# Expert jobs of 160 rows without bias products on TensorE, with bias columns and row folds on GpSimd

## The reference

```python
xb = h[row_tok].reshape(n_blocks, EXPERT_BLOCK, D)      # rows gathered by expert
hid = jnp.dot(xblk, w1[e]) + b1[e]                      # 1024 -> 2048, with a bias
glu = jnp.minimum(hid[:, 0::2], SWIGLU_LIMIT)
lin = jnp.clip(hid[:, 1::2], -SWIGLU_LIMIT, SWIGLU_LIMIT)
act = glu * jax.nn.sigmoid(SWIGLU_ALPHA * glu) * (lin + 1.0)
out = jnp.dot(act, w2[e]) + b2[e]                       # 1024 -> 1024, with a bias
y = zeros((T, D)).at[row_tok].add(out * row_gate)       # scattered back with the gate
```

## Time and profile before

| | |
|---|---|
| median of three runs | 2200.66 us (2197.22 to 2201.60) |
| the profiled execution | 2203.66 us, of which the span from first to last instruction is 2202.1 us |
| TensorE busy in the span | 2050.6 us, 93% |
| DVE, ACT, GpSimd busy | 1600.1, 1296.1 and 423.2 us |
| mean granted TensorE clock | 0.974 |
| loop of jobs | from 675 to about 2170 us |

### The profile page before, as it was taken

How to read it: one execution, slowest core, us unless ns; L and a number is a source line. 1 busy time by engine, 2 the same in 40 slices (tenths; PEclk the granted TensorE clock), 3 DMA queues, 4 the chain that set the end, 5 groups by cost and what they waited for, 6 DMA issues and landing times. The chain is left out here.

```text
span 2202.1 us, 40266 instructions
## 1 busy us (share of the span) xinstructions
PE 2050.6 (93%) x11606; PEld 1763.0 (80%) x11607; DVE 1600.1 (73%) x2206; ACT 1296.1 (59%) x1869; POOL 423.2 (19%) x478
## 2 busy tenths in 40 slices
PE   7999977778957999999999999999999999999994
PEld 6888867777846878889798897979898888979883
DVE  5342176985657677878878787888788797887876
ACT  5221245563436576766757667677667676675765
POOL 3100000220241131221213121132212131121311
PEclk9999989999978999999999999999999999999997
DMA  5221210004247897979889798899898797988978
GB/s 182 61 82 58 67 68 1 11 20 159 96 156 254 278 305 243 352 247 327 287 278 333 237 353 267 297 314 358 253 318 302 257 349 248 334 284 278 331 239 309
DMA packets 260913, 506.10 MB, mean 230 GB/s; under 512 B 34496, under 2 KB 35520, under 8 KB 260566
## 3 DMA queue, kind: packets, MB, share of 16 engines
q1 hardware_dynamic: 243064, 458.05, 60.5%
q0 software_dynamic: 17792, 47.33, 8.8%
q10 hardware_dynamic: 4, 0.02, 0.0%
HBM read 466.10 MB, written 39.22 MB: 229 GB/s over the span
## 5 line engine op out<-in xcount | busy, mean ns | idle before, releaser
L1820 DVE TENSOR_TENSOR wlo<-raw,whi 128x1024 fp32r<-128x1024 f32 x774 | 932.1, 1219 | 75.6 <-ACT whi L1296 67.7
L1296 ACT ACTIVATE whi<-raw 128x1024 fp32r<-128x1024 f32 x775 | 846.1, 1116 | 221.6 <-PE ps L981 162.8
L979 PE MATMUL ps<-xT,whi 128*128 128x320 f32 x1920 | 525.2, 350 | 5.6 <-DMA brow<-brow_d 5.0
L981 PE MATMUL ps<-xT,wlo 128*128 128x160 f32 x1920 | 456.4, 238 | 0.0
L979 PEld LDWEIGHTS ps<-xT,whi 128*128 128x128 f32 x1920 | 364.0, 190 | 10.0 <-issue 6.6
L981 PEld LDWEIGHTS ps<-xT,wlo 128*128 128x128 f32 x1920 | 369.8, 193 | 0.2
L2088 POOL DMA_INDIRECT acc_d<-y,icur x64 | 102.6, 1604 | 947.9 <-ACT y L1330 885.3
L621 PE MATMUL ps<-whi,xT 128*128 128x512 f32 x544 | 216.0, 397 | 0.0
L621 PE MATMUL ps<-whi,aT 128*128 128x512 f32 x512 | 213.1, 416 | 1.3
L623 PE MATMUL ps<-whi,xT 128*128 128x512 f32 x544 | 213.3, 392 | 0.0
L622 PE MATMUL ps<-wlo,xT 128*128 128x512 f32 x544 | 213.1, 392 | 0.0
(11 more groups left out here) (300 smaller groups left out, 3484.4 us busy)
## 6 DMA issues: line engine op xcount, KB each, us to landing
raw<-in_w SPq DMA_DIRECT2D x780, 512.0 KB, 7.4
raw<-in_w_in SPq DMA_DIRECT2D x16, 512.0 KB, 4.7
xs<-in_x SPq DMA_DIRECT2D x8, 512.0 KB, 10.5
raw<-in_w_out SPq DMA_DIRECT2D x8, 512.0 KB, 3.9
mix<-in_x SPq DMA_DIRECT2D x8, 512.0 KB, 4.2
acc_d<-mix SPq DMA_DIRECT2D x8, 512.0 KB, 5.0
h_d<-h SPq DMA_DIRECT2D x8, 512.0 KB, 2.6
mix<-acc_d SPq DMA_DIRECT2D x8, 512.0 KB, 7.5
```

The lines of the kernel that those rows point to most:

```text
L979: pe.matmul(o2, wh[:, a, cols], xT2[:, :, k, 0:JOB_T], start=q == 0 and a == 0, stop=False, skip_group_check=True)
L981: m = pe.matmul(o, wl[:, a, cols], xT2[:, 0, k, 0:JOB_T], start=False, stop=q == QUARTERS - 1 and a == 1, skip_group_check=True)
L1296: act.activation(parted(slot(whis, s)), paired(raw_slot(s), s), ACT.Copy).then_inc(split_hi, 1)
L1820: dve.tensor_tensor(parted(slot(wlos, s)), paired(raw_slot(s), s), parted(slot(whis, s).bitcast(F32)), ALU.subtract).then_inc(split_lo, 1)
```

## The change

It has four parts.

1. In wide jobs the four bias products per c (L984) go. Instead, before the loop, SP loads `b1` once as 32 rows (`b1r`), TensorE turns it in 16 small transposes, and DVE copies the result to `bcolT`, with 1 added to the second half. Per job GpSimd copies one expert's 16 columns to `bcur`. ACT adds the gate's bias inside the sigmoid, which takes two instructions of 160 columns instead of one of 320. DVE gets one more instruction of 320 columns per c, which adds the bias to `lsum`.
2. The bias row for narrow jobs is no longer loaded by SP at the end of its list (nor by ACT the first time) but by GpSimd on its own queue, once the up-projection of the job before is over (`next_bias`).
3. `y_fold` moves from DVE to GpSimd: ACT scales all 64 rows of the second bank into `y` in one instruction, GpSimd copies rows 32 to 63 to `yfold`, then adds them to rows 0 to 31. In GpSimd's list both folds stand ahead of the first scatter.
4. GpSimd reads the next job's expert number from the table (one more register load per job).

The diff, cut:

```diff
+            sp.dma_start(b1r[:, :], b1[0]).then_inc(b1r_in, 16)
...
-                    wait(quarter_used, j * NS + 4 * (DENSE_UNITS + 4))
-                    wait(brow1_in, j * 16 + 16)
-                    sp.dma_start(brow[0:2, 0:2 * FF].bitcast(F32),
-                                 bias_part(en, slice(0, 2 * FF))).then_inc(brow1_in, 16)
...
+            pe.wait_ge(b1r_in, 16)
+            for two in range(2):
+                for i in range(BTILES):
+                    cols = slice(2 * P * i + two, 2 * P * (i + 1) + two - 1, 2)
+                    m = pe.transpose(ps[:, 3, (two * BTILES + i) * NE:(two * BTILES + i + 1) * NE],
+                                     b1r[:, cols], ident[0:NE, 0:NE])
+            m.then_inc(bias_turned, 1)
...
-                        if q == 0:
-                            pe.matmul(o, brow[:, c * UNIT + 256 * odd + P * i:c * UNIT + 256 * odd + P * (i + 1)], ones2[:, 0:JOB_T],
-                                      start=False, stop=False, skip_group_check=True)
...
                     act.wait_ge(sum_taken, j * 8 + 2 * c + 1)
-                    act.activation(sigw[:, :, :], gsum[:, :, :], ACT.Gelu_apprx_sigmoid).then_inc(sig_set, 1)
+                    if c == 0:
+                        act.wait_ge(bcur_set, j + 1)
+                    for i in range(2):
+                        m = act.activation(sigw[:, i, :], gsum[:, i, :], ACT.Gelu_apprx_sigmoid,
+                                           bias=bcur[:, 0, 2 * c + i:2 * c + i + 1])
+                    m.then_inc(sig_set, 1)
...
-                    act.wait_ge(y_set[1], j * 2 + c - 3)
-                    act.activation(yfold[:, c - 4, :], ps[HALF:2 * HALF, out_bank(2, c, 1), :], ACT.Copy,
-                                   scale=gcur[HALF:2 * HALF, 1:2]).then_inc(yfolded, 1)
+                    act.activation(y[0:2 * HALF, 1, (c - 4) * UNIT:(c - 3) * UNIT], ps[0:2 * HALF, out_bank(2, c, 1), :], ACT.Copy,
+                                   scale=gcur[0:2 * HALF, 1:2]).then_inc(yfolded, 1)
...
-            act.wait_ge(quarter_used, 4 * DENSE_UNITS)
-            act.dma_start(brow[0:2, 0:2 * FF].bitcast(F32), bias_part(0, slice(0, 2 * FF))).then_inc(brow1_in, 16)
...
+                if c == 0:
+                    dve.wait_ge(bcur_set, j + 1)
+                dve.tensor_tensor(lsum[:, :, :], lsum[:, :, :],
+                                  bcur[:, 1, 2 * c:2 * c + 2].unsqueeze(2).broadcast_to([P, 2, JOB_T]),
+                                  ALU.add).then_inc(lin_biased, 1)
+                dve.wait_ge(lin_biased, j * 4 + c + 1)
...
+            def next_bias(j, e):
+
+                wait(quarter_used, j * NS + 4 * (DENSE_UNITS + 4))
+                wait(brow1_in, j * 16 + 16)
+                pool.dma_start(brow[0:2, 0:2 * FF].bitcast(F32), bias_part(e, slice(0, 2 * FF))).then_inc(brow1_in, 16)
+                wait(act_set, j * 4 + 4)
+                columns(bass.ds(e, 1))
+                wait(bcur_set, j + 2)
+
+            def y_fold(j, c):
+
+                wait(yfolded, j * 2 + c - 3)
+                cols = slice((c - 4) * UNIT, (c - 3) * UNIT)
+                pool.tensor_copy(yfold[:, c - 4, :], y[HALF:2 * HALF, 1, cols]).then_inc(low_moved, 1)
+                pool.wait_ge(low_moved, j * 2 + c - 3)
+                pool.tensor_tensor(y[0:HALF, 1, cols], y[0:HALF, 1, cols], yfold[:, c - 4, :], ALU.add).then_inc(y_set[1], 1)
+                pool.wait_ge(y_set[1], j * 2 + c - 1)
...
                 pool.tensor_copy(icur[:, :], ikept[:, :]).then_inc(tcur_set, 1)
                 wait(tcur_set, j + 1)
 
+                if blocks == 2:
+                    next_bias(j, e)
+                    y_fold(j, 4)
+                    y_fold(j, 5)
                 for b in ((0, 1) if blocks == 2 else (1, 0)):
+                    if b == 0 and blocks == 1:
+                        pool.sem_inc(low_moved, 2)
+                        next_bias(j, e)
                     if b < blocks:
                         wait(y_set[b], j * 2 + 4)
```

More of the change, by code:

```diff
@@ L81 @@
 B_AV, B_HI, B_HG, B_OUT = 0, 128, 640, 1152
+BTILES = FF // P
 F32 = mybir.dt.float32
@@ L150, in build @@
     tinit = at("tinit", B + 68 * KB, [P, PAD_ROWS, 2])
+    b1r = at("b1r", B + 40 * KB, [NE, 2 * FF])
     hf = at("hf", B, [P, HH, T])
@@ L180, in build @@
     glw = at("glw", B + 55.75 * KB, [P, 2, 2, JOB_T])
+    bcur = at("bcur", B + 58.25 * KB, [P, 2, BTILES])
     yfold = at("yfold", B + 60 * KB, [HALF, 2, UNIT])
+    bcolT = at("bcolT", B + 64 * KB, [P, 2, BTILES, NE])
     R = [B + 72.5 * KB]
@@ L328, in build @@
         rooted, eps_set, brow_zero = sem("rooted"), sem("eps_set"), sem("brow_zero")
-        lin_set, yfolded = sem("lin_set"), sem("yfolded")
+        lin_set, yfolded, low_moved = sem("lin_set"), sem("yfolded"), sem("low_moved")
+        b1r_in, bias_turned, bcolT_set, bcur_set = (
+            sem(n) for n in ("b1r_in", "bias_turned", "bcolT_set", "bcur_set"))
+        lin_biased = sem("lin_biased")
         pool_mark, sync_mark, act_mark = sem("pool_mark"), sem("sync_mark"), sem("act_mark")
@@ L1887, in aT_wide @@
                                   aTh[:, k, 1, 0:HALF].bitcast(F32), ALU.subtract).then_inc(aT_lo, 1)
-            def y_fold(j, c):
-                dve.wait_ge(yfolded, j * 2 + c - 3)
-                dve.scalar_tensor_tensor(out=y[0:HALF, 1, (c - 4) * UNIT:(c - 3) * UNIT], in0=ps[0:HALF, out_bank(2, c, 1), :],
-                                         scalar=gcur[0:HALF, 1:2], in1=yfold[:, c - 4, :],
-                                         op0=ALU.mult, op1=ALU.add).then_inc(y_set[1], 1)
             def job(j, blocks):
@@ L1899, in job @@
                         (hidden if blocks == 1 else hidden_wide)(j, UNIT_END[s - 1])
-                    if blocks == 2 and UNIT_END.get(s - 1, 0) == 4:
-                        y_fold(j, 4)
                     jsplit(j, s + AHEAD)
@@ L1911, in job @@
                 if blocks == 2:
-                    y_fold(j, 5)
                     dve.sem_inc(hid_taken, 4)
@@ L1916, in job @@
                     dve.sem_inc(lin_set, 4)
+                    dve.sem_inc(lin_biased, 4)
             for s in range(4):
                 jsplit(0, s)
+            dve.wait_ge(bias_turned, 1)
+            dve.tensor_copy(bcolT[:, 0, :, :], ps[:, 3, 0:BTILES * NE].rearrange("p (i e) -> p i e", e=NE))
+            dve.tensor_scalar(bcolT[:, 1, :, :], ps[:, 3, BTILES * NE:2 * BTILES * NE].rearrange("p (i e) -> p i e", e=NE),
+                              1.0, None, ALU.add).then_inc(bcolT_set, 1)
             dve.memset(y[:, 1, :], 0.0).then_inc(y_zero, 1)
@@ L2039, in _ @@
                     pool.wait_ge(brow_zero, 2)
+                    pool.dma_start(brow[0:2, 0:2 * FF].bitcast(F32), bias_part(0, slice(0, 2 * FF))).then_inc(brow1_in, 16)
                     link(pool.memset(xg[:, 1, :], 0.0))
@@ L2067, in gather, with columns @@
                                             ).then_inc(gathered, 16)
+            def columns(e):
+                pool.tensor_copy(bcur[:, :, :], bcolT[:, :, :, e].rearrange("p a i o -> p a (i o)")).then_inc(bcur_set, 1)
+            def next_bias(j, e):
[12 more added lines that the diff above has]
+                pool.wait_ge(y_set[1], j * 2 + c - 1)
             def job(j, blocks):
@@ L2074, in job @@
                 load_slots(pool.value_load(jobt[0:1, 1, bass.ds(j + 1, 1)], min_val=0, max_val=NE * JOBS_E - 1))
+                e = pool.value_load(jobt[0:1, 0, bass.ds(j + 1, 1)], min_val=0, max_val=NE - 1)
                 wait(x_turned, j * 4 + 4)
@@ L2107, in _ @@
             pool.wait_ge(y_zero, 1)
+            pool.wait_ge(bcolT_set, 1)
+            columns(slice(0, 1))
+            pool.wait_ge(bcur_set, 1)
             with pool.Fori(0, JOBS, 1) as j:
```

## The result

| | before | changed |
|---|---|---|
| median | 2199.30 us (4 runs, 2197.22 to 2201.60) | 2170.60 us (4 runs, 2168.57 to 2173.04) |
| ratio, 95% interval | | 0.9861 [0.9848, 0.9873] |
| span of the profiled execution | 2202.1 us | 2168.5 us |
| mean granted TensorE clock | 0.974 | 0.974 |
| TensorE, DVE, GpSimd busy | 2050.6, 1600.1, 423.2 us | 2023.1, 1630.9, 534.9 us |

The kernel is 1.4% faster. The forecast was 2186 us, 0.67% faster: right in sign, but with a gain of 14.7 us where 28.7 us were measured. The time lies inside the range only because the range took in the first rival (2166 to 2170 us), which had 20%.

The account below looks back on a forecast made before the run. TensorE, busy 93% of the span, was taken as the bound, full in wide jobs. Terms -27 - 7.7 + 20 + 0.4 = -14.3 us took the profiled 2203.66 to 2189.4 us, a median forecast of 2186 us, range 2167 to 2200.

Parts of the forecast that it names:

- the first rival: Narrow jobs behind wide ones: gathers stay in time, loss only 0 to 4 us, time 2166 to 2170 us; chance 20%.
- The forecast's case: Late gathers cost TensorE 20 us at its turns in narrow jobs; own range 2172 to 2196 us, chance 62%.
- The bias products (-27): Wide jobs' up-projection: removing 240 products from TensorE, 0.11 us each and four at half clock, gains 27 us.
- all of it is on the path, as wide jobs are full: Wide jobs: TensorE is busy throughout, so the bias products' whole 27 us was counted as gain.
- DVE's additions and ACT's sigmoids (0): Wide jobs: four extra instructions per job on each engine fit its idle time and cost nothing.
- The bias row (-7.7): Before wide jobs: GpSimd's earlier issue removes TensorE's three waits, 5.0 us, and 2.7 us at half clock.
- The folds on GpSimd (+20): End of wide jobs: folds ahead of the scatters delay the next narrow job's gathers; loss 20 us, bounds 10 to 44.
- The delay: GpSimd, end of a wide job: the folds make the first scatter 3.3 us later, bounds 2.4 and 5 us.
- everything behind it in GpSimd's list moves along: GpSimd behind the folds: scatters, index load, casts and gathers all shift with the first scatter's 3.3 us.
- the small copies meet fewer splits: GpSimd behind the scatters: its small copies wait less for DVE's splits and give the delay back; within a 20% rival.
- The clock: TensorE's clock stays at 1.0 at 718, saving 2.7 us; the 2.8 us wait at 777.40 is left in.
- The start (+0.4): Before the loop: GpSimd's first row issue ahead of the last table writes, with transposes, copies and `b1r`, loses 0.4 us.

Follow-up runs that it names:

- the row alone: Kernel before the change, with only the bias row issued by GpSimd after the up-projection (bias columns prepared but unused): 2190.04 us, 0.9945 of before.
- the products back: Changed kernel with the bias products back on TensorE in wide jobs, folds and bias row still on GpSimd: 2189.83 us, 0.9940 of before.
- the kernel with three memsets: Changed kernel with folds on VectorE and three GpSimd memsets of 860 columns ahead of each wide job's first scatter: 2174.53 us, 0.9869 of before.

## Why the prediction was wrong

The forecast's case, 20 us lost at the turns, did not happen. The first rival, that the gathers stay in time, nearly did, and mainly by the reason that it gave: the small copies give the delay back. Point by point:

- **The bias products (-27).** Priced right per product (0.11 forecast and measured), but worth 23.3 us: 14 of a job's 16 count. The step "all of it is on the path, as wide jobs are full" failed: a full engine doesn't say that the next wait is far. The first two products had covered a wait for ACT's copy of 1086.15 to 1086.86, and the third group starts no earlier without them (1.35 us for 1.33).
- **DVE's additions and ACT's sigmoids (0).** Right: no wait of TensorE for them, and DVE's share of a wide job rose to 43.41 of 54.80 us.
- **The bias row (-7.7).** 9.3 us alone. But the term isn't additive: with the products gone and the row left with SP the loop is 28.3 us longer than the changed kernel's (1489.4 less 1461.1), since 12 instead of three rows are late and the clock falls more often. The forecast priced the row's waits as they were in the kernel before, and not as they would be after part 1.
- **The folds on GpSimd (+20).** The delay was near, 3.1 us for 3.3, and so were the addition (1.30 us for 1.15) and the slack (1.5 us). The copy was not: 0.99 us in the mean for 0.5. The failed step is "everything behind it in GpSimd's list moves along". The chain from scatter to gather holds three instructions of two columns that wait for VectorE, and the 8 us between the index load and its cast's end became 7.6. Of 3.1 us, 1.9 were left behind the two small copies, 2.1 at the index load, and 1.7 behind the cast. At the landing it was 1.6 us, and that met a slack of 1.5. The forecast read the spread of these copies in the earlier trace rows, and even put "the small copies meet fewer splits" at 20% of chance, but took their time as fixed in the sum. The sum also had no term for what VectorE gains without the folds: TensorE's 0.33 us at step 22 in each of 14 jobs, 4.6 us, against 2.1 us at the turns. Cost: 0, or a gain of some 2 us against the folds on VectorE, which the medians don't tell from none.
- **The clock.** At 718 as forecast it stayed at 1.00. At 771 it fell where it had not before, behind the same wait of 2.8 us; the second narrow job took 38.70 us for 37.14. The forecast had left this as it was.
- **The start (+0.4).** Can't be seen in the spread of 6 us in which the loop's start lies.

The sum of the measured terms in the loop, -23.3 for the products, -9.3 for the row and 0 for the folds, is -32.6 us; the loop is 33.0 us shorter. That is no test of the terms: the row alone, the products back and the changed kernel are steps from one to the next, so their differences have to add up.

That the small copies end with VectorE's splits is read from the trace: all 31 casts to `ikept` of the changed kernel's loop end within 0.06 us of the end of a split (a split ends only each 1.1 us or more), and 29 of 31 casts to `inext`. In these runs it takes hold of instructions that read: the 45 memsets of 1024 columns behind the folds, in the kernels with one and with two of them, all started during a split and took 0.95 or 0.96 us each, and the splits that ran beside a memset alone took 1.21 or 1.22 us. That this is contention for SBUF, and not something else that the two share, wasn't shown by a run here. The Trainium skill, "GPSIMD Engine Reference", section "Key points", says that the two share their SBUF interfaces; the ends of the casts fit that.

Left open: why the clock fell behind the wait of 2.8 us in the changed kernel and not in the kernel before, and which transfers stand ahead of the row on SP's queue. That `aTl` is what the late product of step 22 waits for is read from the traces and the kernel's order; no experiment changed it alone.

## What to carry to other kernels

Before a delay is passed down a queue, look at which links of the chain have a fixed length and which end with an event of another engine: the second kind takes delays up, up to a step, and here passed the next 0.9 us on as 1.7. A placement that fits by such a step, as the changed kernel's does with nothing to spare at ten of 15 turns, is at a cliff: 0.9 us more at the scatter cost 22 us. And when work is taken from a full engine, look at what it covered, at each place where it stood: here a counter coarser than the need cost 6 us, most of it hidden behind two bias products before, and a transfer at the end of a long queue would have taken 28. A change that measures as zero can be two that cancel: the folds cost 2.1 us at one place and gave 4.6 at another, and only the jobs' own stretches show it.

## What the runs showed of the hardware

- A cast of 128x2 on GpSimd took 0.19 us (first row below) and, right behind it beside VectorE's splits, a copy of 128x2 took 1.24 us. This is the kernel with three memsets:

```profile
1148.99 0.19 POOL L2117 CAST ikept<-tnext 128x2 int32<-128x2 f32 x1
1149.12 1.24 POOL L2118 COPY gcur<-tnext 128x2 f32<-128x2 f32 x1
```

- It goes both ways: one of VectorE's splits took 2.18 us beside GpSimd's addition of 32x512, where 1.22 is usual. In the changed kernel's loop 30 splits took over 1.5 us, each of them beside one of the 30 additions, and none did in the kernels with the folds on VectorE:

```profile
1140.73 2.18 DVE L1829 TENSOR_TENSOR wlo<-raw,whi 128x1024 fp32r<-128x1024 f32 x1 [0.75 <-ACT whi L1304]
```

- On GpSimd, over the whole loop, the 30 additions of 32x512 took 1291 ns in the mean and the 30 copies 987 ns.
- A memset of 128x1024 on GpSimd took 0.95 or 0.96 us in all 45 cases beside VectorE's splits, which stretch its copies, and didn't lengthen them.

- A wait shown as 0.19 us of TensorE's idle time lengthened the stage by 0.40 us (33.64 against 33.24 us); its weight load stood idle for 0.39 us ahead of it.
- A row of 16 KB landed in 3.4 to 5.4 us on GpSimd's queue at the moment at which one on SP's queue behind raw slots took 9.54 us.
